# One decoder-layer step on one core: the new values of a gated delta rule as X(V - K S) in place of U - W S, and its decay matrix made on ScalarE from gate rows that a transfer repeats

## The reference

```python
gcum = jnp.cumsum(gc, axis=-1)
decay = jnp.exp(jnp.where(tri, gcum[..., :, None] - gcum[..., None, :], -jnp.inf))
kb = kc * bc[..., None]
a = jnp.where(strict, jnp.einsum('nbhid,nbhjd->nbhij', kb, kc) * decay, 0.0)
rhs = jnp.concatenate([vc * bc[..., None], kb * jnp.exp(gcum)[..., None]], axis=-1)
sol = lax.linalg.triangular_solve(a + eye, rhs, left_side=True, lower=True, unit_diagonal=True)
u, w = sol[..., :DV], sol[..., DV:]
...
v_new = u_i - jnp.einsum('bhck,bhkv->bhcv', w_i, S)
o_i = (jnp.einsum('bhck,bhkv->bhcv', q_i * jnp.exp(g_i)[..., None], S)
       + jnp.einsum('bhij,bhjv->bhiv', qk_i, v_new))
S = (S * jnp.exp(g_last)[..., None, None]
     + jnp.einsum('bhck,bhcv->bhkv', k_i * jnp.exp(g_last[..., None] - g_i)[..., None], v_new))
```

## Time and profile before

| | |
|---|---|
| median of 3 runs | 2325.46 us |
| the runs | 2317.98, 2325.46, 2333.61 us |
| span of the profiled execution | 2317.8 us |
| PE, PEld busy | 2172.3 us (94%), 2081.6 us (90%) |
| DVE, ACT, POOL busy | 983.0 us (42%), 529.0 us (23%), 777.6 us (34%) |
| the chain that ended last, by engine | PE 86%, DVE 6%, ACT 2%, DMA 2% |
| tile stage | 428.3 to about 1006 us |
| tiles begin at | 428.3, 504.0, 576.2, 647.25, 719.35, 790.3, 862.5, 933.4 us |

### The profile page before, as it was taken

One profiled execution on the slowest core, in us unless ns is written; L12 is line 12 of the kernel. 1 busy time (PEld: TensorE's weight loads), 2 busy tenths in 40 slices (PEclk: granted clock), 3 DMA queues, 4 the chain that ended last, 5 costly groups with the idle time before them and its releaser, 6 DMA issues.

```text
span 2317.8 us, 36058 instructions
## 1 busy us (share of the span) xinstructions
PE 2172.3 (94%) x13799; PEld 2081.6 (90%) x13799; DVE 983.0 (42%) x1678; ACT 529.0 (23%) x1125; POOL 777.6 (34%) x340
## 2 busy tenths in 40 slices
PE   5999998799999999989989989679999999999997
PEld 4999997688888888889969989679999999999996
DVE  5554034343444434420134860554344334334336
ACT  4332152233233332321112221420000000000003
POOL 2434447222120221112123434433443443443444
PEclk9999999899999999989779999789999999999998
DMA  4323323421222221135265422321111111111113
GB/s 148 102 74 102 95 83 99 118 81 48 61 77 72 81 66 43 44 101 161 65 191 166 158 76 78 124 66 46 45 45 45 45 45 45 49 45 42 54 37 150
DMA packets 225073, 189.54 MB, mean 82 GB/s; under 512 B 24491, under 2 KB 200171, under 8 KB 224962
## 3 DMA queue, kind: packets, MB, share of 16 engines
q1 hardware_dynamic: 213074, 179.62, 25.0%
q10 hardware_dynamic: 11904, 8.52, 1.2%
HBM read 142.07 MB, written 47.06 MB: 82 GB/s over the span
## 4 chain that ended last, share of the span: by engine, by line
PE 86%; DVE 6%; ACT 2%; DMA 2%; issue 2%; SPq 1%; POOL 1%; DVEq 0%; ACTq 0%; POOLq 0%
PE psum L1258 22%; PE psum L830 14%; PE psum L1038 12%; PE psum L1325 10%; PE psum L908 7%; PE psum L1250 4%; PE psum L1268 4%; PE psum L1023 2%; PE psum L996 2%; PE psum L1012 1%; DMA brw<-s_br 1%; DVE xs L2213 1%; PE psum L1119 1%; PE psum L1001 1%; PE psum L840 1%
## 5 line engine op out<-in xcount | busy, mean ns | idle before, releaser
L734 POOL TENSOR_TENSOR wsp<-raw,kc 128x1024 fp32r<-128x1024 f32 x145 | 349.1, 2407 | 1434.1 <-PE psum L1038 473.8
L1258 PE MATMUL psum<-actD,wsp 128*128 128x352 f32 x3168 | 515.3, 323 | 0.9 <-DVE actD L2219 0.9
L1258 PEld LDWEIGHTS psum<-actD,wsp 128*128 128x128 f32 x3168 | 509.4, 189 | 1.0 <-DVE actD L2219 1.0
L737 POOL TENSOR_TENSOR wsp<-raw,wsp 128x1024 fp32r<-128x1024 f32 x145 | 364.1, 2511 | 11.4
L830 PE MATMUL psum<-actT,wsp 128*128 128x352 f32 (+1 forms) x1944 | 314.7, 323 | 0.0
L830 PEld LDWEIGHTS psum<-actT,wsp 128*128 128x128 f32 (+1 forms) x1944 | 306.6, 185 | 5.2
L1038 PE MATMUL psum<-actT,wsp 128*128 128x352 f32 x1728 | 304.8, 334 | 0.0
L1038 PEld LDWEIGHTS psum<-actT,wsp 128*128 128x128 f32 x1728 | 287.1, 196 | 0.1
L2268 DVE TENSOR_TENSOR accT<-accT,psum 128x352 f32<-128x352 f32 x504 | 242.3, 520 | 50.4 <-PE psum L1325 50.4
L1325 PE MATMUL psum<-fT,wsp 128*128 128x352 f32 x1512 | 250.4, 323 | 0.4 <-DVE accT L2268 0.4
L1325 PEld LDWEIGHTS psum<-fT,wsp 128*128 128x128 f32 x1512 | 244.5, 188 | 0.7 <-DVE accT L2268 0.7
(11 more groups left out here) (386 smaller groups left out, 2348.1 us busy)
## 6 DMA issues: line engine op xcount, KB each, us to landing
raw<-in_w_in SPq DMA_DIRECT2D x100, 256.0 KB, 4.0
raw<-in_w_ffn_in SPq DMA_DIRECT2D x88, 256.0 KB, 3.1
gat<-s_gate SPq DMA_DIRECT2D x12, 1056.0 KB, 5.1
raw<-in_w_ffn_out SPq DMA_DIRECT2D x44, 256.0 KB, 2.8
s_gate<-gst SPq DMA_DIRECT2D x48, 176.0 KB, 1.8
s_qkv<-y SPq DMA_DIRECT2D x12, 528.0 KB, 3.0
brw<-s_br SPq DMA_DIRECT2D x3, 2112.0 KB, 9.7
raw<-in_w_branch SPq DMA_DIRECT2D x24, 256.0 KB, 6.3
```

Source lines behind the costliest of these rows:

```text
L734: pool.tensor_tensor(wsp[:, slot, 0], raw[:, slot], ones.unsqueeze(1).to_broadcast([P, KT, P]), ALU.mult).then_inc(w_hi, 1)
L737: pool.tensor_tensor(wsp[:, slot, 1], raw[:, slot], wsp[:, slot, 0].bitcast(F32), ALU.subtract).then_inc(w_lo, 1)
L1258: mm = pe.matmul(psum[:, bank, 0:CH], wsp[:, slot, a, k, :], actD[:, h, k, CH * c:CH * c + CH], start=(k == 0 and q == 0), stop=(k == KT - ...
```

## The change

Four things are done, in the tile stage and just ahead of it.

First, in place of U and W: at a new step `KS` behind the first gate chunk TensorE computes k S in bank 7, VectorE scales it to `ks` and subtracts it from `vb`, in place. At `UN` TensorE computes X vb alone, and ScalarE copies the result as `vn`. `kbe`, W, the copies of U and W, W S and VectorE's subtraction from U are gone. Second, q S (`PO`) is computed right behind the last level of X, ahead of `S` 4. Third, `SO` stands ahead of `V` 4 and `S` 5. Fourth, the decay matrix: the cumulative decays `gcm` and the per-token factor are transposed once in the preparation (2 transposes, one copy on ScalarE, two stores of 16 KB to `s_row`), and for each tile SyncE loads one row of both, repeated over all 128 partitions, into `rowb` (512 KB written), a tile ahead, behind the store of the tile's second gate chunk. ScalarE makes the differences with four `Relu` operations, one a head, and takes the exponential of the result in one more. Step `DEC` leaves TensorE altogether, and GpSimd's `ug` and `bi` are gone.

```diff
-    TILE = ("KV", ("S", 0), "DEC", "KK", ("G", 0), ("T", 0), "INV", ("V", 0), ("Y", 1), ("S", 1), ("X", 1),
+    TILE = ("KV", ("S", 0), "DEC", "KK", ("G", 0), "KS", ("T", 0), "INV", ("V", 0), ("Y", 1), ("S", 1), ("X", 1),
...
-            ("S", 4), ("D", 0), "UW", ("G", 3), ("F", 0), "PO", ("T", 4), ("V", 4), ("S", 5), "SO", ("T", 5),
+            "PO", ("S", 4), ("D", 0), "UN", ("G", 3), ("F", 0), ("T", 4), "SO", ("V", 4), ("S", 5), ("T", 5),
...
+                    if j == 0 and c == 1 and not last:
+                        sp.wait_ge(at_st, 4 * t + 2)
+                        load_rows(t + 1)
...
         sp.wait_ge(o_st, 64)
+        sp.wait_ge(rw_cp, 2)
+        for x in range(2):
+            sp.dma_start(s_row[x].rearrange("t (h i) -> (t h) i", h=BH), rowt[:, x, :]).then_inc(rw_st, 16)
...
         load_tile(0, 0)
+        sp.wait_ge(rw_st, 32)
+        load_rows(0)
...
-                elif step == "DEC":
-                    pe.matmul(psum[:, 7, :], k_gt, ug[:], start=True, stop=True).then_inc(e_gt, 1)
-                    pe.matmul(psum[:, 5, :], ones, bi[:], start=True, stop=True).then_inc(e_br, 1)
+                elif step == "KS":
+                    pe.wait_ge(kq_ok, t + 2)
+                    mm4(7, k, lambda h: st[:, h, :], e_ks)
...
-                elif step == "UW":
+                elif step == "PO":
+                    pe.wait_ge(c_x, 6 * t + 6)
+                    mm4(5, q, lambda h: st[:, h, :], e_o1)
+                elif step == "UN":
                     pe.wait_ge(c_xt, 6 * t + 6)
+                    pe.wait_ge(r_ok, t + 1)
                     mm4(6, lambda h: xt[:, h, :], lambda h: vb[:, h, :], e_u)
-                    mm4(5, lambda h: kbe[:, h, :], lambda h: xt[:, h, :], e_w)
-                elif step == "PO":
-                    mm4(7, lambda h: wt[:, h, :], lambda h: st[:, h, :], e_p1)
-                    mm4(5, q, lambda h: st[:, h, :], e_o1)
...
-                    act.activation(dec[:].rearrange("p h i -> p (h i)"), psum[:, 7, :], ACT.Exp).then_inc(dec_ok, 1)
+                    for h in range(BH):
+                        mm = act.activation(dec[:, h, :], rowb[:, 0, h, :], ACT.Relu, scale=-1.0,
+                                            bias=gcm[:, bass.ds(t, 1), h])
+                    mm.then_inc(dec_ok, 1)
+                    act.wait_ge(dec_ok, 2 * t + 1)
+                    act.activation(dec[:].rearrange("p h i -> p (h i)"), dec[:].rearrange("p h i -> p (h i)"), ACT.Exp,
+                                   scale=-1.0).then_inc(dec_ok, 1)
...
-                elif step == "UW":
-                    copy((e_u, t + 1), uu[:].rearrange("p h i -> p (h i)"), psum[:, 6, :], c_u)
-                    copy((e_w, t + 1), wt[:].rearrange("p h i -> p (h i)"), psum[:, 5, :], c_w)
+                elif step == "UN":
+                    copy((e_u, t + 1), vn[:].rearrange("p h i -> p (h i)"), psum[:, 6, :], vn_ok)
...
-                    dve.tensor_tensor(at[:], at[:], head4(5), ALU.mult).then_inc(at_st, 1)
+                    dve.tensor_tensor(at[:], at[:], rowb[:, 1], ALU.mult).then_inc(at_st, 1)
...
+                elif step == "KS":
+                    dve.wait_ge(e_ks, t + 1)
+                    dve.tensor_tensor(ks[:], head4(7), bc_c(per(Q_BKE, t)), ALU.mult).then_inc(ks_ok, 1)
+                    dve.wait_ge(ks_ok, t + 1)
+                    dve.tensor_tensor(vb[:], vb[:], ks[:], ALU.subtract).then_inc(r_ok, 1)
```

More of the change, by code:

```diff
@@ L129, in build @@
     egl = sb("egl", [P, NT + 1, BH])
+    gcm = sb("gcm", [P, NT, BH])
     tmp = sb("tmp", [P, 6, NT + 1, BH])
@@ L219, in build @@
     Q_BETA, Q_G, Q_BK, Q_BKE, Q_KD, Q_EG, Q_RK, Q_RQ = range(8)
-    vb, kbe, kd = (sb(n, [P, BH, P], on=cC) for n in ("vb", "kbe", "kd"))
-    ug, bi, mrk = (sb(n, [P, BH, P], on=cC) for n in ("ug", "bi", "mrk"))
+    vb, ks, kd = (sb(n, [P, BH, P], on=cC) for n in ("vb", "ks", "kd"))
+    rowb = sb("rowb", [P, 2, BH, P], on=cC)
+    rowt = sb("rowt", [BH * NT, 2, P], on=cC)
+    mrk = sb("mrk", [P, BH, P], on=cC)
     dec, decm, kqd, at = (sb(n, [P, BH, P], on=cC) for n in ("dec", "decm", "kqd", "at"))
@@ L543, in _, with load_rows @@
         sp.wait_ge(o_st, 64)
+        sp.wait_ge(rw_cp, 2)
+        for x in range(2):
+            sp.dma_start(s_row[x].rearrange("t (h i) -> (t h) i", h=BH), rowt[:, x, :]).then_inc(rw_st, 16)
         sp.sem_inc(c_ob, 1)
+        def load_rows(t):
+            sp.dma_start(rowb[:].rearrange("p x h i -> p x (h i)"),
+                         s_row[:, bass.ds(t, 1), :].rearrange("x a n -> (a x) n").partition_broadcast(P)).then_inc(rw_in, 16)
         for s in range(2):
@@ L761, in _ @@
                 pool.wait_ge(dm_ok, t + 1)
-                pool.tensor_tensor(ug[:], bc_h(k_le), bc_c(per(Q_G, t)), ALU.mult).then_inc(ug_ok, 1)
                 pool.tensor_tensor(mrk[:], bc_h(k_le), bc_c(per(Q_RK, t)), ALU.mult).then_inc(mrk_ok, 1)
-                pool.wait_ge(kq_ok, t + 1)
-                pool.tensor_tensor(bi[:], bc_h(ident), bc_c(per(Q_BK, t)), ALU.mult).then_inc(bi_ok, 1)
                 for j in (1, 2):
@@ L900, in _ @@
                 mm.then_inc(mt, 1)
+        pe.wait_ge(pp, 15)
+        pe.wait_ge(rw_cp, 1)
+        pe.transpose(psum[0:BH * NT, 7, 0:P], gcm[:].rearrange("p t h -> p (t h)"), ident)
+        pe.transpose(psum[0:BH * NT, 7, P:2 * P], par[:, Q_BK, 0:NT, :].rearrange("p t h -> p (t h)"), ident).then_inc(rw_mm, 1)
         pe.wait_ge(mc, 1 + 4)
         pe.wait_ge(st0, 3)
+        pe.wait_ge(rw_cp, 2)
         def mm4(bank, lhs, rhs, done, w=P):
@@ L1518, in _ @@
                     act.activation(dst[0:NS, NT, :], psum[0:NS, 5, 36 * x + 32:36 * x + 36], ACT.Exp).then_inc(pa, 1)
+                act.activation(gcm[:], psum[:, 5, 0:32].rearrange("p (t h) -> p t h", h=BH), ACT.Copy).then_inc(rw_cp, 1)
                 act.wait_ge(pp, 11)
@@ L1525, in _ @@
                 act.activation(mout[:, s, :] if v == 0 else mv[:, s, :], psum[:, 5 + j % 2, :], ACT.Copy).then_inc(mc, 1)
+        act.wait_ge(rw_mm, 1)
+        act.activation(rowt[:].rearrange("n x i -> n (x i)"), psum[0:BH * NT, 7, 0:2 * P], ACT.Copy).then_inc(rw_cp, 1)
         for c in range(3):
@@ L1900, in dve_tile @@
                     dve.wait_ge(e_tk, t + 1)
-                    dve.tensor_tensor(kbe[:], head4(5), bc_c(per(Q_BKE, t)), ALU.mult)
                     dve.tensor_tensor(kd[:], head4(5), bc_c(per(Q_KD, t)), ALU.mult).then_inc(kd_ok, 1)
```

33 lines of the change are left out of this document (13 added, 20 removed).

## The result

The changed kernel takes 2350.65 us (median of four runs, 2347.69 to 2355.27). The kernel before takes 2321.72 us (four runs, 2316.45 to 2333.61). The ratio is 1.0121 with a 95% interval of 1.0089 to 1.0153: 1.2% slower. The profiled execution took 2350.47 us, its span is 2348.7 us, 30.9 more than before.

A forecast was written before the change was run, and what follows sets the result against it. TensorE, busy 94%, was taken as the bound, its saving lost to waits on ScalarE and VectorE. Tiles 1 to 7 17.8 us plus tile 0 1.6 made 19.4; on 2325.5 that gave 2345 us, range 2335 to 2380.

The forecast's parts named there:

- The clock: Tile stage: TensorE's granted clock stays at 1.00 despite the new idle stretches, with tiles of 74.5 us.
- bound of 1%: Whole kernel: 1%, 23 us, hardly told from no change; slower beyond it 0.38, within 0.58, faster 0.04.
- The start of a tile: From `dec` to `S` 1: four Relus delay `decm` 1.22 us, `ks` and `vb` add more; `S` 1 is 2.54 late.
- The end of a tile: Last level of X to `T` 5: gain 0 (loss 0.3 to gain 0.1), TensorE idling about 2.2 us ahead of `T` 5.
- The first tile and what lies ahead of it: Stores ahead plus tile 0: 0.8 + 2.5 - 1.7 = 1.6 us more (0 to 3.5), 1.7 gained on a VectorE operation.
- tiles 1 to 7: Tile stage behind tile 0: 2.54 us more a tile, 17.8 us in all (15 to 22).
- My sign of being wrong: Tile stage: tiles shorter than 72 us, `Relu` spacing far from 0.3, or a clock below 0.95.
- rival B: New idle stretches: TensorE's clock falls, about 3 us each; 2369 us at one a tile; chance 0.29 in some or all tiles.
- B in one place of each tile: Start or end of each tile: one clock fall a tile, 24 us on top, 2369 us.
- Rival A: Tile start and end: all hidden, TensorE's saving up to 21.8 us kept, 2304 us; chance 0.07 including half of it.
- Rival C: Tile 0: `rowb`'s row load comes late, costing 1 to 5 us once, 2348 us; counted inside the forecast's 0.61.

The follow-up runs named there:

- e4: Changed kernel with VectorE's masks of levels 3 to 5 moved behind its copy for `S` 1, nothing left out: 2327.05 us, ratio 1.0043.
- e1: Kernel before with the decay part of the change alone (rows from memory, ScalarE's decay matrix; U and W stay): 2347.29 us, ratio 1.0122.
- e2: Kernel before with the delta rule and its order alone, decay matmuls kept: 2327.71 us, ratio 1.0046.
- e12: Kernel before with only VectorE's level masks 3 to 5 moved behind its copy for `S` 1: 2324.13 us, ratio 1.0016.
- e8: Changed kernel with unread matmuls filling both gaps, 13 ahead of `S` 1, 12 ahead of `T` 5: 2341.56 us; stage 0.36 us shorter per us less at low clock.
- e6: Changed kernel with VectorE's masks 3 to 5 behind its copy for `S` 1 and `G` 4 ahead of `T` 5: 2307.62 us, ratio 0.995.
- e7: e6 with ScalarE making the Relus and the Exp ahead of its copy for `S` 0: 2303.86 us, ratio 0.9927.
- e3: Changed kernel with 13 unread matmuls behind `Y` 1, in the gap ahead of `S` 1: 2346.06 us, ratio 1.0122.
- e5: Changed kernel with `G` 4 moved ahead of `T` 5, nothing added or left out: 2349.60 us, ratio 1.0138.

## Why the prediction was nearly right in time and too low on the clock

The forecast, 2345 us or 0.8% slower, lies 0.4 points below the measured 1.2%; the range holds it. By the bound of 1% the ratio of 1.0121 is slower, to which I had given 0.38, and not within 1%, 0.58; its interval, from 1.0089, does not settle that. Part of the closeness is luck. I had added 19.4 us, and the medians differ by 28.9, the profiled spans by 30.9. The 2345 comes within 5.7 of the measured time because it stood on a median of three runs that a fourth brought down by 3.7, and because what follows the tile stage took 6.4 less.

**The start of a tile: right.** `decm` was to be 1.22 us late (0.95 to 1.49) and is 1.34: the four Relus take 1.27 us in all, so with 0.295 for the last the spacing is 0.325 where I took 0.295. The Trainium skill, ScalarE: Activation LUTs, section What ACT_TABLE_LOAD costs, gave an estimated 0.29; the trace has it 0.035 above. (The spacings of 0.20 and 0.38 give bounds of 0.94 and 1.48, not 0.95 and 1.49.) `KS` was to wait 0.95 us and waits 0.84. `S` 1 was to be 2.54 late and is 2.57, with an idle stretch of 2.13 where I had about 2.5, as the transposes of `T` 0 start 0.27 later than before and not at the same place. e4 and e1, e2 confirm the mechanism: the delays of the two parts add up, and relieving VectorE of three masks removes the wait.

**The end of a tile: right.** The gain from the last level of X to `T` 5 was to be 0 (-0.3 to 0.1) and is 0.23; `T` 5's wait was to be 2.2 and is 2.04.

**The first tile and what lies ahead of it: right in the stores, the rest chance.** I had 1.6 us. The stage begins 3.2 us late and tile 0 takes 2.6 more, 5.7 in all. The two stores take 0.80 us as expected. The small operation of VectorE takes 0.33 us where it took 1.85, because it starts just ahead of the end of one of GpSimd's (both end at 437.84); and a fall of 6.8 us lies in this tile. But 2.4 of the 3.2 us arise ahead of any instruction that the change touches: there VectorE's operations on 36 or 72 columns end together with GpSimd's on 1024, one each. One of them, in the kernel after and GpSimd's beside it, then in the kernel before and in e12, whose code is unchanged there, and in e4, which has the changed kernel's code there:

```profile
402.18 2.40 DVE L1900 SCALAR_TENSOR_TENSOR tmp<-tmp 128x36 f32<-128x36 f32 x1
402.18 2.35 POOL L755 TENSOR_TENSOR wsp<-raw,wsp 128x1024 fp32r<-128x1024 f32 x1
```

```profile
401.03 0.20 DVE L1877 SCALAR_TENSOR_TENSOR tmp<-tmp 128x36 f32<-128x36 f32 x1
402.11 2.40 DVE L1877 SCALAR_TENSOR_TENSOR tmp<-tmp 128x36 f32<-128x36 f32 x1
403.30 0.20 DVE L1900 SCALAR_TENSOR_TENSOR tmp<-tmp 128x36 f32<-128x36 f32 x1
```

It takes 2.4 us or 0.20, in either code, so these 2.4 us are chance of an execution and not shown to be an effect of the change: the stage begins at 431.54 in e12, and at 430.89 in e4. The 6.4 us that the unchanged rest of the program took less lie within the 1301.8 to 1313.7 us that it takes in the fourteen kernels; what sets that spread is not shown.

**The clock: the step that failed.** For tiles 1 to 7 I had 17.8 us and the trace has 31.5. By e8's price the clock accounts for all of the 13.7 between them (41.0 us low in these tiles at 0.36 are 14.8). Of the 41.0, 30.8 lie behind the wait ahead of `S` 1 and 10.2 at two turns of the loop, where e12 shows that a fall comes without the change too. I had forecast tiles of 74.5 us at a clock of 1.00; tiles 1 to 7 take 73.42 to 77.73, and the stage has 0.96. My sign of being wrong, a clock below 0.95, was set too low to catch this. I had weighed this as rival B, with a chance of 0.29, and let the clock of 1.00 in the tiles before speak against it, although those tiles had no wait of 2 us within themselves. It fell in every tile. The sentence that the tile stage's clock is 1.00 before also passed over the first 8.6 us of the stage, which ran at the lower level. The rule of the Trainium skill, TensorE: Matmul & The Clock Gate, section A second HAM failure mode: psum-queue depth-cycling, that short idle stretches between groups of matmuls can make the clock swing, pointed the right way, and this trace agrees with it at `S` 1 (0.50 at 682 to 684 behind 2.13 us of idle time) but not at `T` 5 (1.00 behind 2.04). What kept the forecast close is that B's price was too high: I took 6 us at the lower clock and 3 us lost; the ten falls last 4.8 us on average, and cost 1.7, probably since part of the slower work lies ahead of waits that would have come anyway. B in one place of each tile was to give 2369 us. The truth lies between the forecast and B: B's mechanism at little more than half its price.

**Smaller points.** Rival A, all kept, was to give 2304: wrong for this kernel, but its conditions were named rightly (the copy ahead of the levels, the softmax covered); with these two met e6 comes to 2307.6 and e7 to 2303.9. Rival C did not come: nobody waits for `rowb`. And I had set the sum on a median 7.7 us above the profiled span; the profiled execution after lies 1.8 us above its own span, so that distance was the spread of the runs and no constant.

## What to carry to other kernels

Work taken off the busiest engine counts only if no other engine's chain has become the longer one: list, for each place where work leaves, what the next instruction waits for, and move off that chain whatever is needed later (three masks, one gate chunk and one ScalarE step turned 1.2% slower into 0.7% faster here). Where TensorE runs dense, an idle stretch of 2 us costs its length and can bring a fall of the clock on top. With one of two such stretches closed here, the falls came at the other (e3, e4) or grew longer there (e5); close them all, then measure. When a change loses, try its parts and its repairs on both kernels: here the half that looked like the larger saving cost the most alone, and the repairs were worth nothing without the change.
